# A two-block transformer kernel on one core: small stages of the second block by tokens and transfers, modulation tiles laid out anew

## The reference

```python
# first block, layers 0 and 1
mod = silu(c) @ ada_w[layer] + ada_b[layer]          # shift, scale, gate of 3 sub-layers
x = post(x, swiglu_ffn(pre(x)));  x = post(x, mixer(pre(x)));  x = post(x, swiglu_ffn(pre(x)))
# mixer: a short convolution in layer 0, block-sparse attention (NSA, 16 heads) in layer 1
# pre:  x * rsqrt(mean x^2) * g * (1+scale) + shift;   post: x + w*gate * (y * rsqrt(mean y^2) * g)

# second block, l = 0 and 1
mod = silu(c2) @ w_ada[l] + b_ada[l]
h = rms_norm(x, norm1) * (1+sc1) + sh1
q, k, v, g, u, vs, p, gate_cols = split(h @ w_in)    # 512,512,1024,1024,1024,1024,1024,3072 columns
q, k = rotary(q), rotary(k) * 128**-0.5              # halves swapped, one with the sign turned
o = (q k^T * decay) @ v                              # 4 heads, chunks of 128
y_ret = silu(g) * (o * rsqrt(mean over a head's 256 of o^2))
y_sgu = gelu(u) * (tril(w_s) @ (rms_norm(gelu(vs)) * v_gain) + b_s)   # mixes tokens of a chunk
y_pool = (trailing means - p) @ w_pool, bias, scale
x = x + gt1 * ((sum_n sigmoid(gate_n) * (y_n @ w_branch[n])) @ w_out)
x = x + gt2 * (relu(h2 @ w_ff1)^2 @ w_ff2)
out = rms_norm(x)                                    # after l = 1
```

## Time and profile before

| what | value |
|---|---|
| time, median of 3 | 2252.71 us |
| the profiled execution: time, span | 2253.69 us, 2251.8 us |
| PE busy, 17514 instructions | 2152.6 us (96%) |
| DVE, ACT, POOL busy | 1589.8 us (71%), 1015.5 us (45%), 200.4 us (9%) |
| chain that ended last | PE 82%, DVE 10%, DMA 4%, ACT 2%, issue 1% |
| granted TensorE clock, mean | 0.967 |
| moved by DMA | 495.41 MB, mean 220 GB/s |

### The profile page before, as it was taken

The page is one execution under the profiler, slowest core; times in us unless marked ns, Lnnn a source line. Parts: engine busy times, 40 slices in busy tenths (PEclk is TensorE's granted clock), DMA queues, the critical chain, the costliest instruction groups (busy, mean ns, idle before and its releaser), DMA issues.

```text
span 2251.8 us, 40284 instructions
## 1 busy us (share of the span) xinstructions
PE 2152.6 (96%) x17514; PEld 2114.3 (94%) x17514; DVE 1589.8 (71%) x1901; ACT 1015.5 (45%) x1082; POOL 200.4 (9%) x330
## 2 busy tenths in 40 slices
PE   5999998999999998899999999999999999999997
PEld 5999998998999997689999999999999999998997
DVE  6666888877767787677888344768898544667655
ACT  3434635434434455554345453345445444335442
POOL 0010111111001111211100000000111000001000
PEclk9999999999889996999999999999999999999999
DMA  9788575897579952248975445464996545546553
GB/s 333 253 290 275 200 249 192 302 332 258 165 254 330 329 198 75 85 151 277 333 245 187 158 134 177 160 230 161 357 378 223 176 132 169 169 160 215 198 183 106
DMA packets 265072, 495.41 MB, mean 220 GB/s; under 512 B 17088, under 2 KB 146496, under 8 KB 264768
## 3 DMA queue, kind: packets, MB, share of 16 engines
q1 hardware_dynamic: 230192, 366.47, 49.0%
q0 software_dynamic: 34704, 126.37, 14.9%
HBM read 491.73 MB, written 1.05 MB: 219 GB/s over the span
## 4 chain that ended last, share of the span: by engine, by line
PE 82%; DVE 10%; DMA 4%; ACT 2%; issue 1%; SPq 0%; DVEq 0%; POOL 0%; ACTq 0%
PE PA L485 9%; PE PA L487 9%; PE PA L486 9%; PE PB L485 8%; PE PB L487 8%; PE PB L486 8%; PE PY L485 6%; PE PY L487 6%; PE PY L486 6%; DVE wlo L1331 3%; ACT whi L986 1%; PE PY L520 1%; PE PY L516 1%; PE PY L518 1%; DMA raw<-ffn_w_in 1%
## 5 line engine op out<-in xcount | busy, mean ns | idle before, releaser
L1331 DVE TENSOR_TENSOR wlo<-raw,whi 128x2048 fp32r<-128x2048 f32 x335 | 766.4, 2299 | 380.3 <-ACT whi L986 379.7
L986 ACT ACTIVATE whi<-raw 128x2048 fp32r<-128x2048 f32 x335 | 636.0, 1907 | 456.3 <-DMA raw<-ffn_w_in 195.9
L485 PE MATMUL PA<-opA_hi,whi 128*128 128x256 f32 x1536 | 437.5, 285 | 9.1 <-DVE opA_lo L1381 7.5
L487 PE MATMUL PA<-opA_hi,wlo 128*128 128x256 f32 x1536 | 435.5, 284 | 0.0
L486 PE MATMUL PA<-opA_lo,whi 128*128 128x256 f32 x1536 | 434.4, 283 | 0.0
L485 PE MATMUL PY<-opB_hi,whi 128*128 128x256 f32 x1344 | 377.5, 281 | 4.6 <-DVE wlo L1331 3.9
L487 PE MATMUL PY<-opB_hi,wlo 128*128 128x256 f32 x1344 | 375.8, 280 | 0.0
L486 PE MATMUL PY<-opB_lo,whi 128*128 128x256 f32 x1344 | 375.7, 280 | 0.0
L485 PE MATMUL PB<-opA_hi,whi 128*128 128x256 f32 x1280 | 361.6, 283 | 4.6 <-DVE wlo L1331 2.4
L487 PE MATMUL PB<-opA_hi,wlo 128*128 128x256 f32 x1280 | 360.1, 281 | 0.0
L486 PE MATMUL PB<-opA_lo,whi 128*128 128x256 f32 x1280 | 359.0, 280 | 0.0
(11 more groups left out here) (301 smaller groups left out, 3381.0 us busy)
## 6 DMA issues: line engine op xcount, KB each, us to landing
raw<-ffn_w_in SPq DMA_DIRECT2D x176, 512.0 KB, 5.2
scr<-adat POOLq DMA_DIRECT2D x160, 512.0 KB, 6.2
raw<-w_in SPq DMA_DIRECT2D x144, 512.0 KB, 4.6
raw<-w_ff SPq DMA_DIRECT2D x128, 512.0 KB, 4.7
raw<-ffn_w_out SPq DMA_DIRECT2D x88, 512.0 KB, 4.9
adaw<-adat POOLq DMA_DIRECT2D x80, 512.0 KB, 6.3
raw<-w_branch SPq DMA_DIRECT2D x48, 512.0 KB, 4.4
raw<-a_w_in SPq DMA_DIRECT2D x24, 512.0 KB, 4.5
```

The costliest lines, as they stand in the source:

```text
L485: nc.tensor.matmul(o_, w1, rhs(xh), start=start, stop=False, skip_group_check=True)
L487: return nc.tensor.matmul(o_, w2_, rhs(xh), start=False, stop=stop, skip_group_check=True)
L986: AC(whi[slot][:, 0:w], raw[slot][:, 0:w], ACT.Copy).then_inc(hi_ready, 1)
L1331: TT(wlo[slot][:, 0:w], raw[slot][:, 0:w], whi[slot][:, 0:w].bitcast(F32), ALU.subtract).then_inc(lo_ready, 1)
```

## The change

1. Modulation tiles: ffn00 works off 40 instead of 32, conv 8 instead of 16, ffn10 32 instead of 48, and 16 go into the NSA stage, 8 of them around the products q0 and q1 and 8 beside nsa_out. While NSA uses the other slabs' memory these 16 go through two slabs only (`SL`, `BEFORE`). Inside an FFN all tiles are used up by input step 10, and `mods` stands ahead of the last two output chunks.
2. Boundaries: `accy` is summed in two DVE instructions of 512 columns instead of five of 256, and PE sums its two halves.
3. v and vs are computed with tokens on the partitions (`tokens512`): the activations are the stationary operand, the weights move, 512 columns at a time, 24 matmuls for a chunk instead of 48. The transposes of v and vs go; the norm of vs is by partition on ACT (squares with a running sum, a scaled copy), its gain goes into the DVE instruction after the token mix (8 instead of 4).
4. The rotation's swapped halves are fetched by two transfers that POOL starts, instead of a product.
5. Sums of squares of o: POOL adds the two tiles of a head, PE sums and spreads them in 4 matmuls, ACT takes the root of 1024 columns, DVE four reciprocals of 256 columns.
6. w_s comes transposed from the host. PA and PB change places from p0 on.

```diff
+        for _name, _count, _run in (("first", 16, 16), ("ffn00", 24, 40), ("conv", 24, 8), ("ffn01", 40, 40), ("cmp", 0, 8),
+                                    ("ffn10", 24, 32), ("nsa", 32, 16), ("ffn11", 40, 40), ("ff0", 48, 48), ("ff1", 8, 8)):
...
+        nsa0 = RUN["nsa"][0]
+        SL = [g % SLABS for g in range(nsa0)] + [g % 2 for g in range(16)] + [(2 + g) % SLABS for g in range(256 - nsa0 - 16)]
+        BEFORE = [max([h for h in range(g) if SL[h] == SL[g]], default=-1) for g in range(256)]
-            return sum(1 for h in range(16, g + 1) if h % SLABS == g % SLABS)
+            return sum(1 for h in range(16, g + 1) if SL[h] == SL[g])
...
-                    nc.tensor.matmul(PB[:, 0, :], onesD, accy[:], start=True, stop=False)
+                    for m in range(2):
+                        nc.tensor.matmul(PB[:, 0, :], onesD, accy[:, m, :], start=m == 0, stop=False)
...
+                def tokens512(name, buf, before=None):
+                    nonlocal c
+                    take(buf)
+                    for h in range(2):
+                        slot = c % RING
+                        pe.wait_ge(lo_ready, c + 1)
+                        for kk in range(4):
+                            k = 4 * h + kk
+                            if before:
+                                before(k)
+                            wh, wl = whi[slot][:, 512 * kk:512 * kk + 512], wlo[slot][:, 512 * kk:512 * kk + 512]
+                            for j in range(2):
+                                o_ = flat[buf][:, 512 * j:512 * j + 512]
+                                xh, xl = oph["A"][:, k, j * P:j * P + P], opl["A"][:, k, j * P:j * P + P]
+                                nc.tensor.matmul(o_, xh, wh, start=k == 0, stop=False, skip_group_check=True)
+                                nc.tensor.matmul(o_, xh, wl, start=False, stop=False, skip_group_check=True)
+                                last = nc.tensor.matmul(o_, xl, wh, start=False, stop=k == KT - 1, skip_group_check=True)
+                        last.then_inc(multiplied, 1)
+                        c += 1
+                    by(buf, "S", f"b{l}.{name}")
...
-                need(pe, "S", f"b{l}.k")
-                for t in range(8):
-                    last = nc.tensor.matmul(PY[:, t, :], rotm, t3(X[0], 8)[:, t, :], start=True, stop=True)
...
-                take("Y")
-                need(pe, "S", f"b{l}.v1")
...
+                tokens512("s1", "B")
+                take("A")
+                need(pe, "G", f"b{l}.osum")
                 for h in range(4):
-                    need(pe, "S", f"b{l}.osq{h}")
-                    for e in range(2):
-                        for j in range(2):
-                            last = nc.tensor.matmul(flat["B"][:, 2 * h + j:2 * h + j + 1], tmp8[:, 2 * h + e, j * P:j * P + P],
-                                                    onesD[:, 0:1], start=h == 0 and e == 0 and j == 0, stop=e == 1,
-                                                    skip_group_check=True)
+                    last = nc.tensor.matmul(PA[:, h, :], onesD, t3(rr, 4)[:, h, :], start=h % 2 == 0, stop=True, skip_group_check=True)
-                by("B", "S", f"b{l}.osd")
-                group("s1", "A")
-                take("B")
-                need(pe, "V", f"b{l}.odiag")
-                for h in range(4):
-                    last = nc.tensor.matmul(PB[:, h, :], onesD, hdiag[:, h, :], start=h % 2 == 0, stop=True, skip_group_check=True)
-                S(last, f"b{l}.ospread")
-                by("B", "S", f"b{l}.rr")
+                by("A", "S", f"b{l}.osd")
-                ssq(f"b{l}.v")
-                group("h00", "A")
-                group("h01", "B")
...
-                group("v0", 2, "A", half(1, 0), ACT.Copy)
-                group("v1", 3, "B", half(1, 1), ACT.Copy)
+                def tokens(i, h):
+                    return X[i].rearrange("p (j e) -> p j e", j=2)[:, :, 512 * h:512 * h + 512]
+                def group_tokens(name, i, buf, dst, func):
+                    prep_to(c + 2 * i + 4)
+                    act.wait_ge(multiplied, c + 2 * i + 2)
+                    S(AC(dst, flat[buf].rearrange("p (j e) -> p j e", j=2), func), q_ + name)
...
-                S(AC(t3(rr, 4), PB[:], ACT.Copy), q_ + "rr")
+                S(AC(t3(rr, 4), PA[:], ACT.Sqrt, bias=epsc[:], scale=D / 256.0), q_ + "osd")
+                need(act, "S", q_ + "s1")
+                vt = X[3].rearrange("p (j e) -> p j e", j=2)
+                st = X[5].rearrange("p (j e) -> p j e", j=2)
+                for j in range(2):
+                    S(AC(vt[:, j, :], st[:, j, :], ACT.Square, accum_out=osd[:, j:j + 1]), q_ + "vsq")
+                need(act, "S", q_ + "vsq")
+                S(AC(osd[:, 2:4], osd[:, 0:2], ACT.Sqrt, bias=epsc[:], scale=1.0 / D), q_ + "vsd")
+                group("p0", 10, "B", half(1, 0), ACT.Copy)
+                need(act, "V", q_ + "vr")
+                for j in range(2):
+                    S(AC(vt[:, j, :], st[:, j, :], ACT.Copy, scale=osd[:, 4 + j:5 + j]), q_ + "vntok")
+                group("p1", 11, "A", half(1, 1), ACT.Copy)
+                prep_to(c + 26)
...
-                    need(dve, "S", f"{sub}.ysq0")
-                    v = S(TT(accy[:], tmp8[:, 0, :], tmp8[:, 1, :], ALU.add))
-                    for m in range(2, KT - 2):
-                        need(dve, "S", f"{sub}.ysq{m // 2}")
-                        own(v)
-                        v = S(TT(accy[:], accy[:], tmp8[:, m, :], ALU.add), f"{sub}.acc")
+                    for q in range(1, 3):
+                        need(dve, "S", f"{sub}.ysq{q}")
+                        settle()
+                        S(TT(accy[:], tmp8[:, 0:2, :] if q == 1 else accy[:], tmp8[:, 2 * q:2 * q + 2, :], ALU.add), f"{sub}.acc")
...
-                    ada_to(r0 + min(rn, max(0, p_ - c0 - a_ + 1) * rn // (FFN_AT["out", FFN_STEPS - 2] - a_)))
+                    ada_to(r0 + min(rn, max(0, p_ - c0 - a_ + 1) * rn // (FFN_AT["in", FFN_STEPS - 1] - a_)))
...
-                        if j < FFN_STEPS - 1:
+                        if j < FFN_STEPS - 3:
                             some(p_)
+                        elif j == FFN_STEPS - 3:
+                            ada_to(r0 + rn)
+                            mods(name)
...
+            prep_to(c + 3)
+            ada_to(nsa0 + 2)
             prep_to(c + 4)
             inverse("11")
             for g in range(2):
                 if g:
+                    ada_to(nsa0 + 6)
                 zevac(f"q{g}", ("AB", "Y")[g], scale=DH ** -0.5)
+                if g == 0:
+                    ada_to(nsa0 + 4)
                 prep_to(c + 5 + 2 * g)
+            ada_to(nsa0 + 8)
...
             out_split(15)
+            prep_to(CH["nsa_out"] + 3)
+            ada_to(nsa0 + 12)
+            prep_to(CH["nsa_out"] + 4)
+            ada_to(nsa0 + 16)
+            mods("nsa")
...
                 own(S(TT(tmp8[:], X0, cos_.unsqueeze(1).broadcast_to([P, 8, T]), ALU.mult)))
-                need(dve, "T", q_ + "rot")
-                own(S(TT(X0, PY[:], sin_.unsqueeze(1).broadcast_to([P, 8, T]), ALU.mult), q_ + "rot"))
+                dve.wait_ge(swapped, 32 * (l + 1))
...
+                prep_to(c + 22)
-                own(S(nc.vector.reciprocal(osd[:], osd[:])))
                 for h in range(4):
-                    for j in range(2):
-                        S(TS(hdiag[:, h, j * P:j * P + P], ident, osd[:, 2 * h + j:2 * h + j + 1], float(D), ALU.mult, ALU.mult),
-                          q_ + "odiag")
-                prep_to(c + 22)
-                need(dve, "S", q_ + "rr")
+                    v = S(nc.vector.reciprocal(rr[:, T * h:T * h + T], rr[:, T * h:T * h + T]))
+                    if h == 1:
+                        need(dve, "S", q_ + "vsd")
+                        S(nc.vector.reciprocal(osd[:, 4:6], osd[:, 2:4]), q_ + "vr")
+                        prep_to(c + 23)
+                settle()
+                prep_to(c + 24)
...
+                merge(0, 0, "B", c + 28)
+                merge(0, 1, "A", c + 30)
-                for g in range(4):
-                    v = S(TT(tmp8[:, 2 * g:2 * g + 2, :].rearrange("p e (n t) -> p (e n) t", n=2),
-                             PY[:, 2 * g:2 * g + 2, :].rearrange("p e (n t) -> p (e n) t", n=2),
-                             bs[:, g, :].unsqueeze(1).broadcast_to([P, 4, P]), ALU.add), q_ + "mix")
+                for k in range(KT):
+                    v = S(STT(tmp8[:, k, :].rearrange("p (n t) -> p n t", n=2), PY[:, k, :].rearrange("p (n t) -> p n t", n=2),
+                              V("vnorm", 8 * l + k, 1), bs[:, k // 2, :].unsqueeze(1).broadcast_to([P, 2, P]), ALU.mult, ALU.add),
+                          q_ + "mix")
...
             for l in range(2):
+                need(pool, "S", f"b{l}.k")
+                X0, X5 = t3(X[0], 8), t3(X[5], 8)
+                for u in range(2):
```

(9 more changed lines are left out.)

149 lines of the change are left out of this document (52 added, 97 removed).

## The result

The changed kernel takes 2224.56 us (median of 4 runs, 2222.52 to 2228.03) against 2252.78 (2252.36 to 2256.30): a ratio of 0.9874, 95% interval 0.9859 to 0.9890. The forecast was 2209, with a range up to 2223: the direction was right, two thirds of the gain came, and the time lies outside the range. The profiled execution took 2222.52 with a span of 2220.6, so 31.2 us of span are gone, where the sum said 43.5; the median of the runs lies another 2 above it.

A forecast was written before the change was run, and what follows sets the result against it. The kernel was taken as one line of PE work with short breaks. Mixing stages 34.8 plus boundaries 19.7 less NSA 11.0 gave 43.5 us off 2253.7, so 2210.2, median 2209; range 2199 to 2223.

The forecast's parts named there:

- Nothing waits: Mixing stages: POOL can send the swapped halves at about 1210, DVE wants them at 1222.4, so the transfers cost nothing.
- 00, 01, 02 and 10: Boundaries where PE waits less for accy: gains of 1.7, 8.4, 3.5 and 3.9 us.
- NSA: Tiles through two slabs make the gates 6.5 us later and accy at the end 4.5: cost 11.0, bounds 6 and 16.
- r10: Mixing stages: the token mix in 8 DVE instructions instead of 4 makes PE wait 1.1 us more before r10.
- v1's wait: Layer 0: PE stands 4.8 us before v1, bringing half clock; v1 ends at 1230.7 instead of 1229.3, a loss of 1.2.
- The rotation: Its 3.45 us product leaves PE: gain 0 in layer 0, 2.4 us in layer 1 with v1's own saving.
- the last of the signs: Mixing stages: the prediction is wrong if POOL's transfers of the halves land after DVE asks for them.
- I take 0.75, near the first: Mixing stages: 512-column matmuls, priced from the fp32 256-column row, save 0.75 us a group, 1.5 for s0 and s1.
- ff0: First wide FFN: change 0; its slices 29 and 30 moved 357 and 378, cited as room on the queues.
- At 12, 2.2: Boundary 12: two tiles and mods go from the end, as at 10, a gain of 2.2 us.
- one-column piece: Piece between s0 and s1, 16 one-column products: its 4.20 us go, and 2.3 of half clock behind it.
- PE runs into lower halves: Rival: h00, g0 and p1 meet late DVE lower halves, half the mixing gain goes; 2226 us, chance 0.14.

The follow-up runs named there:

- x10: The changed kernel with the loads of w_s, b_s and w_pool sent three groups later; 2220.2 us.
- x2: The changed kernel with the rotation's product back on PE in place of the two transfers of swapped halves; 2219.8 us.
- x11: The changed kernel with 20 idle products of 128 columns on PE before v1 of the first mixing stage; 2225.4 us.
- x5: The changed kernel with another order on DVE and ACT around v1, lower and upper halves ahead of the rotation's work; 2217.3 us.
- x3: The changed kernel with the 16 modulation tiles of the NSA stage moved into ffn10; 2209.4 us.
- x9: The changed kernel with 8 of the first wide FFN's 48 modulation tiles worked off in ffn11 instead; 2225.3 us.
- x8: The changed kernel with NSA's tiles in ffn10, the new order around v1, three loads later and 8 ff0 tiles in ffn11; 2196.6 us, ratio 0.9735.
- x12: The kernel of x8 with the rotation's product on PE again; 2198.1 us.
- x4: The changed kernel with only its mixing stages new: modulation tiles, mods and accy as in the kernel before; 2228.8 us.
- x1: The changed kernel run again with no edit; 2226.6 us.

## Why the prediction was wrong

The step that failed is the price of the rotation's swapped halves: "Nothing waits" put it at nothing, and it cost layer 1 4.3 us in this trace and more in the others of this stage. Several terms were mis-sized beside it.

The mechanism was right at 00, 01, 02 and 10 (within 0.8 of the first trace each, closer than the old kernel's own traces agree at 00 and 10, so partly luck), in NSA (both parts within 0.5; that the table has 9.0 is scatter between the two), in the pieces that go between g1 and the output (mix0 from g0 to the output's start: 16.6 less, forecast 16.8), at r10 (0.75 more wait instead of 1.1), and at v1's wait (5.05 instead of 4.8). 12.3 us of gain are missing in the profiled execution, in these steps:

- "Half a MB takes 3.6 us alone and 6.4 among six", and then "Nothing waits". This is the step that failed. I looked at POOL's queue and at DVE's need in layer 0 (12 us later), and not at what SP sends at that moment, w_s, b_s and w_pool with the chunks, nor at layer 1, where DVE is there after 8.7 us. The halves took 8.4 and 10.7 us in layer 1 and 8.7 and 11.5 in layer 0, where they landed 0.1 us before DVE wanted them: that nothing waited for them there was luck. Step "The rotation", layer 1, said +2.4; with g0's wait and the half clock behind it (12.66 us from a group's first start to its last instead of 11.3) it came to -1.9: 4.3 lost, and 6 to 7 in the other traces, where the stretch is 2 to 3 us longer. x10 and x2 show the cause, each by taking one of the two parties away. It was the last of the signs that I had named: DVE waited 2.65 for the halves.
- In layer 0 the wait was right, but not its price. I let v1 end at 1230.7; with 2.8 us at half clock the stretch from v0 to g0 became 30.2 us where my sum had 28.9: 1.4. (The sum's loss of 1.2 doesn't follow from its own numbers either: 1230.7 is 1.4 behind the 1229.3 that it names, and 1.1 behind g0's start.) x11 shows that the stand does it, x5 that the order on DVE and ACT makes the stand. Other traces (x3, x9) have v1's group at 12.8, as I had let it take, so this miss differs by execution.
- "I take 0.75, near the first". Matmuls of 512 columns are 0.231 apart, not 0.216 to 0.226, and save 0.2 a group. 0.8 instead of 3.0 for s0 and s1 of both layers: 2.2. The two-pass fp32 record was the wrong neighbour.
- ff0, taken as untouched: 2.4, and 2.4 to 6.2 over the nine traces of the new mixing stages with 48 tiles there. It stood at the edge of what the queues carry, and I used those very slices as proof of room. That fewer tiles mend it is shown (x8, x9, x12: 199.2 to 199.7 with 40); why the changed kernels are late there in every trace and the old one, with as many tiles, in neither, is open. The tiles' layout (x4) and the halves (x2) are excluded.
- At 12, 2.2: the wait went, but the stretch also holds what follows NSA's stand of 6.76 at half clock; without that stand it is 200.3 (x3). Against the old kernel's second trace, 206.2, nothing is missing here.
- Layer 1's one-column piece was cheaper before the change than layer 0's (3.5 us from start to start instead of 4.2, and 1.5 at half clock instead of 2.4), and I took layer 0's for both: 1.5.
- At b00 PE waited 2.05 instead of 0.71: 1.3. The same boundary had 1.00 in x1 and 0.44 in x5, so this differs by execution.

These are 15.3, and 00, 01, 02 and 10 together gave 1.1 less than forecast: 16.4. Against them stand 2.0 in NSA and 0.7 at r10. That leaves 13.7, 1.4 more than is missing, which I can't place. The rival "PE runs into lower halves" (2226) had the mechanism and nearly the time, with a chance of 0.14; it named h00, g0 and p1, of which g0 came, in layer 1, and neither of the others did. My argument against it, three chunks ahead, counted a landing of usual length. The range was too narrow for the same reason: each bound was taken in its own stage, none for several stages running late on one cause.

## What to carry to other kernels

Before a transfer is priced at nothing, list every transfer in flight at that moment, whichever engine starts it, with its landing time there, and what stands behind its waiter on an in-order engine. A stand of PE costs its length and can cost half the clock on what follows (up to 2.8 us behind one of 5.05 here), so the order ahead of a wait can be worth more than the wait. A stage whose queues are full has no room to lend, even if PE doesn't wait in the one trace at hand. Two traces of the old kernel, taken first, would have shown which stretches are fit to be forecast to 1 us.

## What the runs showed of the hardware

A wait doesn't always cost clock: 2.54 at the boundary into mix1 left it at 1.00 in one trace, 2.77 left it there in x3, and 2.79 in the changed kernel brought 0.66 over the next 5 us. 20 idle products in a stand of 5 us kept it at 1.00.

Two transfers of half a MB within the core took 8.4 and 10.7 us beside SP's chunks and the three loads, and 5.7 and 7.6 beside the chunks alone (x10).

In NSA a long half-clock stretch covers the first part of the units. Stretches of the changed kernel's units and of the kernel without tiles in NSA (the granted clock is the number behind the engines'):

```profile
880.00:885.00 5.00, 5.00 (x33) 3.38 (x34) 3.69 (x12) 3.08 (x13) 0.85 (x1) 0.50 0.00 0
886.00:891.00 5.00, 4.28 (x46) 2.86 (x44) 4.45 (x11) 3.02 (x12) 1.08 (x2) 1.00 0.02 3
```

```profile
873.00:878.00 5.00, 4.23 (x47) 2.77 (x45) 4.60 (x15) 3.72 (x15) 1.36 (x2) 0.98 0.00 0
```

It began at 865.4 before, 2 us ahead of the first scores behind the gates, and at 848.0 after, 10 us ahead of them, both 37.5 long. That it began earlier doesn't explain the shorter units: its length differs by execution, 27.3 in the second trace of the kernel before, 23.9 in x3, 20.5 to 44.4 over all fourteen traces, with the units at 73.0 to 76.7. What sets its end is open.
